# Gate and up of an encoder's feed-forward chunks computed transposed, with the inverse rms applied later

## The chip, the cores and the metric

One core of a Trainium2 chip. The metric is the device time of one execution in microseconds (us); lower is better.

## The reference

Two layers over x of shape (1, 256, 1024) in float32. Each layer has two feed-forward blocks with a mixer (spatial gating and windowed attention) between them:

```python
def _rmsnorm(x, g):
    inv = rsqrt(mean(x * x, axis=-1) + EPS)
    return (x * inv) * g

def _swiglu(h, w_in, w_out):          # w_in 1024 x 5632, w_out 2816 x 1024
    gate, up = split(h @ w_in, 2, axis=-1)
    return (silu(gate) * up) @ w_out

for l in range(2):
    x = x + 0.5 * _swiglu(_rmsnorm(x, ffn1_norm[l]), ffn1_w_in[l], ffn1_w_out[l])
    ...                               # mixer: x = x + concat(A, B) @ w_mix_out[l]
    x = x + 0.5 * _swiglu(_rmsnorm(x, ffn2_norm[l]), ffn2_w_in[l], ffn2_w_out[l])
```

## The kernel before, in words

**Arithmetic.** Every float32 operand of a large product is split in a high part (rounded to the matmul type, L464 for weights) and a low part (the rest, L689). `products` (L994) makes three matmuls for each product: high x by high w (L997), high x by low w (L998), low x by high w (L1000). x (transposed, gained, not yet divided by its rms) is the stationary operand, in pieces of 128 tokens; the weights stream, 512 columns at a time.

**Weights.** They come in units of 128 x 2048 (1 MB). SP loads a unit into one of three `raw` buffers (`load`, L293), when the low part of the unit three positions earlier is made. ScalarE (ACT) makes `w_hi`, VectorE (DVE) `w_lo`, in six slots. A chunk of the feed-forward block is 256 of the 2816 inner columns; there are 11. It has two `in` units (each with gate and up columns of four of the eight k tiles) and one `out` unit.

**A feed-forward block** (`ffn` on each engine: L510 ACT, L767 DVE, L1038 PE), four times in the kernel. For chunk c and token half t, PE computes gate and up side by side in PSUM bank `U[t]` (`enter`, L1039: 24 matmuls of 512 columns). ACT takes silu of the gate with the inverse rms as its scale (`silu`, L486), DVE multiplies by up and the inverse rms (`mul`, L705). The result h has tokens on partitions, but the next product wants it the other way: PE transposes it (`transpose_h`, L1049 to L1053: four 128 x 128 for a chunk), ACT and DVE take the high and low part (`take_hT`, L490 and L711), and `leave` (L1055) multiplies by the `out` unit into `acc` (24 matmuls of 512). PE's order for chunk c is: both halves of `enter(c)` with the transposes of h(c-1) in the middle, then `leave(c-1)`. At the end of a block come the transposes of h(10) (two before `leave(9, 0)`, two before `leave(9, 1)`), the residual (`residual`, L714, scale 0.5, L734), and the transposes of the new x (L1035), which are begun as soon as x of token half 0 is there (L1107).

**Around it.** POOL computes the inverse rms (`inverse_rms`, L405, L402 and L403) and, at the start, loads small rows from its own DMA queue (L417, L419). In the first block of layer 0, PE transposes these rows (`other_rows`, L1205 to L1209) in the middle of `enter(1, 0, ...)`, behind a wait for them. In layer 1, POOL loads `ws`, `sgain` and `sinks` (L442 to L444) behind the last inverse rms of layer 0. Orders on all engines are written out by hand.

Of the kernel before, what the change touches and what calls it, by code (L numbers as in the profile page):

```python
# [15 lines left out]
F32 = mybir.dt.float32  # L16
# [3 lines left out]
ALU = mybir.AluOpType  # L20
# [69 lines left out]
def encoder(nc, x, ffn1_norm, ffn1_w_in, ffn1_w_out, mix_norm, w_mix_in, sgu_norm, sgu_w, sgu_b,  # L90
# [18 lines left out]
    RELS = 2 * S - 1  # L109
    bias_rows = nc.dram_tensor("bias_rows", (NH, P, RELS), F32, kind="Internal").ap()  # L110

    with ExitStack() as ctx:
# [14 lines left out]
        xT_hi = sb("xT_hi", [P, KT, S], F32R)  # L127
        xT_lo = sb("xT_lo", [P, KT, S], F32R)
# [17 lines left out]
        kT_lo = hT_hi[:, 0, :, :].rearrange("p t (g n) -> p t g n", n=P)  # L146
        gv = sb("gv", [P, 2, MIX_A])
# [28 lines left out]
        U = [bank("U0"), bank("U1")]  # L176
        acc = [[bank("C0"), bank("C1")], [bank("D0"), bank("D1")]]
        C0, C1 = acc[0]
        TR = [bank("TR0"), bank("TR1")]
# [25 lines left out]
        h_done = sem("h_done")  # L205
        hT_psum = sem("hT_psum")
# [67 lines left out]

        def n_tran(L, q, t, half):

            return L * 12 + (4 * q + 2 * t + half + 1)
# [15 lines left out]
        def _(sp):  # L293
# [8 lines left out]
            def load_in(L, f, c, u, j=0):  # L302
                def parts(dst):
                    d = dst.rearrange("p (k g n) -> p k g n", k=4, g=2)
                    for g in range(2):
                        cols = bass.ds(j * (2 * FC) + (g * DFF + c * FC), FC)
                        yield d[:, :, g, :], w_in[f][bass.ds(L, 1), :, 4 * u:4 * u + 4, cols][0]
                load(L, pos_in(f, c, u), parts, j)
# [75 lines left out]
        def _(pool):  # L384
# [23 lines left out]

            def norm(L, name, c0, groups, n):
# [5 lines left out]
            inverse_rms(0, 0, 1)  # L415
            for r0, v in ((48, q_norm), (50, k_norm)):
# [22 lines left out]
            for L in range(DEPTH):  # L439
# [13 lines left out]
                for q in (2, 3) if L < DEPTH - 1 else (2,):  # L453
                    inverse_rms(L, q, 0)
                    inverse_rms(L, q, 1)
# [3 lines left out]
        def _(act):  # L459
# [16 lines left out]
            def silu(L, f, c, t, j=0):  # L476
                if t == 0:
                    act.wait_ge(gu_ready, n_gu(L, f, c, j))
                else:
                    act.wait_ge(units_used, n_used(L, pos_in(f, c, 1), j))  # L480
                if c == 0:
                    act.wait_ge(inv_done, n_inv(L, 2 * f, t))
                else:

                    act.wait_ge(h_done, n_ffn(L, f, c - 1, t, j))
                act.activation(gate[:, t, :], U[t][:, 0:FC], ACT.Silu, scale=inv[:, t:t + 1]).then_inc(silu_done, 1)  # L486

            def take_hT(L, f, c, t, j=0):
                act.wait_ge(hT_psum, n_ffn(L, f, c, t, j))
                act.activation(hT_hi[:, c % 2, :, t * P:(t + 1) * P],  # L490
                               TR[t][:, 0:FC].rearrange("p (k n) -> p k n", k=2), ACT.Copy).then_inc(hT_hi_done, 1)

# [17 lines left out]
            def ffn(L, f, after):  # L510

                def chunk(c, j=0):
                    if c > 0:
                        silu(L, f, c - 1, 1, j)
                    split(L, pos_in(f, c + 1, 0), j)
                    if c > 0:
                        take_hT(L, f, c - 1, 0, j)
                        take_hT(L, f, c - 1, 1, j)
                    silu(L, f, c, 0, j)
                    split(L, pos_in(f, c + 1, 1), j)  # L520
                    split(L, pos_out(f, c), j)
                chunk(0)
                with act.Fori(0, 4) as j:
                    chunk(1, j)
                    chunk(2, j)
                chunk(9)
                silu(L, f, 9, 1)
                split(L, pos_out(f, 10))
                take_hT(L, f, 9, 0)
                take_hT(L, f, 9, 1)  # L530
                silu(L, f, 10, 0)
                if after is not None:
                    split(L, after[0])
                silu(L, f, 10, 1)
                take_hT(L, f, 10, 0)
# [7 lines left out]
                take_hT(L, f, 10, 1)  # L543
# [133 lines left out]
        def _(dve):  # L677
# [24 lines left out]
            def mul(L, f, c, t, j=0):  # L702
# [611 lines left out]
```

## Time and profile before

| | us |
|---|---|
| median of 3 runs (918.36 to 919.03) | 918.51 |
| the profiled execution, its own time | 918.79 |
| its span | 917.0 |
| PE busy in the span | 911.9 |
| DVE busy | 524.3 |
| ACT busy | 441.9 |
| POOL busy | 54.1 |

The span is from the first to the last instruction that the profile shows; the rest of the time lies outside of it. The granted clock of TensorE is full in each of the 40 slices of the page. Matmuls are pipelined: a 128 x 512 one lasts 0.39 us in the records, but the next starts 0.23 us after it, so starts, not durations, are what to read of PE.

### The profile page before, as it was taken

Reading aid. Unit: us, or ns where it says so; the run is one execution under the profiler, and the core shown is the slowest. Engines: PE = TensorE matmul, PEld = TensorE weight load, DVE = VectorE, ACT = ScalarE, POOL = GpSimd, SP = SyncE. Lnnn points to the kernel's source line nnn. Section 1 sums busy time; section 2 is a strip of 40 time slices with the busy share of each in tenths; the row PEclk is TensorE's granted clock in tenths of the full one; section 3 lists DMA queues with packets and bytes.
Section 4 is the critical chain, followed back from the end, with each engine's and each line's share of the span. In section 5 each row is a group of like instructions: output and inputs, shape, how many; then the busy total and the mean of one; then the engine's idle time right before and its main releaser. Section 6 shows DMA issues by size and latency. Waiting matters only on the chain.

```text
span 917.0 us, 12240 instructions
## 1 busy us (share of the span) xinstructions
PE 911.9 (99%) x4422; PEld 751.7 (82%) x4422; DVE 524.3 (57%) x631; ACT 441.9 (48%) x524; POOL 54.1 (6%) x112
## 2 busy tenths in 40 slices
PE   9999999999999999999999999999999999999998
PEld 7888888887788888888888888888877888888886
DVE  5644554477967445455466445445689574554542
ACT  6444443457856345345254443443677473443530
POOL 2400000111100000000010000000110100000000
PEclk9999999999999999999999999999999999999999
DMA  8999999843174664654456645645431665564531
GB/s 281 279 195 258 177 219 249 222 139 138 61 261 160 223 214 137 224 188 154 160 201 206 231 162 182 230 149 184 138 138 48 229 204 209 184 230 153 186 118 46
DMA packets 119582, 168.88 MB, mean 184 GB/s; under 512 B 5948, under 2 KB 98424, under 8 KB 119544
## 3 DMA queue, kind: packets, MB, share of 16 engines
q1 hardware_dynamic: 117536, 163.47, 51.9%
q0 software_dynamic: 1504, 4.73, 7.5%
q8 instruction: 26, 0.43, 0.2%
q10 hardware_dynamic: 504, 0.16, 0.1%
q14 instruction: 12, 0.10, 0.0%
HBM read 165.19 MB, written 3.14 MB: 184 GB/s over the span
## 4 chain that ended last, share of the span: by engine, by line
PE 96%; DVE 2%; DMA 1%; issue 0%; ACT 0%; SPq 0%; DVEq 0%
PE U L997 19%; PE U L1000 19%; PE U L998 19%; PE C L997 6%; PE C L1000 6%; PE C L998 6%; PE D L997 5%; PE D L998 5%; PE D L1000 5%; PE TR L1052 2%; PE TR L1035 1%; DVE sc L856 1%; PE D L1179 1%; PE TR L1135 1%; DMA raw<-in_ffn_w_in_dram 1%; DVE w_lo L689 0%
## 5 line engine op out<-in xcount | busy, mean ns | idle before, releaser
L689 DVE TENSOR_TENSOR w_lo<-raw,w_hi 128x2048 fp32r<-128x2048 f32 x150 | 340.1, 2289 | 116.5 <-ACT w_hi L464 116.5
L997 PE MATMUL U<-w_hi,xT_hi 128*128 128x512 f32 (+1 forms) x784 | 307.9, 393 | 0.1
L464 ACT ACTIVATE w_hi<-raw 128x2048 fp32r<-128x2048 f32 x150 | 283.4, 1918 | 49.8 <-DMA raw<-in_ffn_w_in_dram 35.2
L1000 PE MATMUL U<-w_hi,xT_lo 128*128 128x512 f32 (+1 forms) x784 | 302.5, 386 | 0.0
L998 PE MATMUL U<-w_lo,xT_hi 128*128 128x512 f32 (+1 forms) x784 | 301.9, 385 | 0.0
L1000 PEld LDWEIGHTS U<-w_hi,xT_lo 128*128 128x128 f32 x784 | 147.3, 188 | 30.3
L997 PEld LDWEIGHTS U<-w_hi,xT_hi 128*128 128x128 f32 x784 | 147.4, 188 | 28.6 <-DVE xT_lo L750 0.3
L998 PEld LDWEIGHTS U<-w_lo,xT_hi 128*128 128x128 f32 x784 | 147.6, 188 | 27.9
L490 ACT ACTIVATE hT_hi<-TR 128x256 fp32r<-128x256 f32 x88 | 29.4, 382 | 242.9 <-PE TR L1052 242.9
L711 DVE TENSOR_TENSOR hT_lo<-TR,hT_hi 128x256 fp32r<-128x256 f32 x88 | 33.5, 419 | 167.6 <-ACT hT_hi L490 167.6
L486 ACT ACTIVATE small<-U,inv 128x256 f32<-128x256 f32 x88 | 41.8, 475 | 114.6 <-PE D L1000 78.0
L705 DVE SCALAR_TENSOR_TENSOR small<-U,inv,small 128x256 f32<-128x256 f32 x88 | 42.0, 477 | 63.2 <-ACT small L486 62.8
L997 PE MATMUL D<-w_hi,hT_hi 128*128 128x512 f32 x176 | 69.2, 393 | 0.0
L997 PE MATMUL C<-w_hi,hT_hi 128*128 128x512 f32 x176 | 68.9, 391 | 0.0
L998 PE MATMUL D<-w_lo,hT_hi 128*128 128x512 f32 x176 | 68.6, 390 | 0.0
L998 PE MATMUL C<-w_lo,hT_hi 128*128 128x512 f32 x176 | 68.5, 389 | 0.0
L1000 PE MATMUL D<-w_hi,hT_lo 128*128 128x512 f32 x176 | 55.6, 389 | 0.0
L1000 PE MATMUL C<-w_hi,hT_lo 128*128 128x512 f32 x176 | 54.3, 390 | 0.0
L1000 PEld LDWEIGHTS D<-w_hi,hT_lo 128*128 128x128 f32 x176 | 33.0, 188 | 7.0
L1000 PEld LDWEIGHTS C<-w_hi,hT_lo 128*128 128x128 f32 x176 | 33.0, 188 | 6.9
L998 PEld LDWEIGHTS C<-w_lo,hT_hi 128*128 128x128 f32 x176 | 33.1, 188 | 6.7
L997 PEld LDWEIGHTS C<-w_hi,hT_hi 128*128 128x128 f32 x176 | 33.0, 188 | 6.7
(121 smaller groups left out, 706.2 us busy)
## 6 DMA issues: line engine op xcount, KB each, us to landing
raw<-in_ffn_w_in_dram SPq DMA_DIRECT2D x168, 512.0 KB, 4.7
raw<-in_ffn_w_out_dram SPq DMA_DIRECT2D x88, 512.0 KB, 5.2
raw<-in_w_mix_in_dram SPq DMA_DIRECT2D x28, 512.0 KB, 4.7
raw<-in_w_mix_out_dram SPq DMA_DIRECT2D x16, 512.0 KB, 3.6
raw<-in_ffn_w_in_dram SPq DMA_DIRECT2D x16, 256.0 KB, 4.7
bias_rows<-brow POOLq DMA_DIRECT2D x8, 255.5 KB, 11.3
bias<-bias_rows POOLq DMA_DIRECT2D x8, 192.0 KB, 6.1
xs<-in_x_dram SPq DMA_DIRECT2D x2, 512.0 KB, 5.5
```

The source lines that it names most:

```text
L464: act.activation(w_hi[:, p % SLOTS, :], raw[:, p % RAW, :], ACT.Copy).then_inc(hi_ready, 1)
L486: act.activation(gate[:, t, :], U[t][:, 0:FC], ACT.Silu, scale=inv[:, t:t + 1]).then_inc(silu_done, 1)
L490: act.activation(hT_hi[:, c % 2, :, t * P:(t + 1) * P], TR[t][:, 0:FC].rearrange("p (k n) -> p k n", k=2), ACT.Copy).then_inc(hT_hi_done, 1)
L689: dve.tensor_tensor(w_lo[:, p % SLOTS, :], raw[:, p % RAW, :], w_hi[:, p % SLOTS, :].bitcast(F32), ALU.subtract).then_inc(lo_ready, 1)
L705: dve.scalar_tensor_tensor(out=h[:, t, :], in0=U[t][:, FC:2 * FC], scalar=inv[:, t:t + 1], in1=gate[:, t, :], op0=ALU.mult, op1=ALU.mult). ...
L711: dve.tensor_tensor(hT_lo[:, c % 2, :, cols], TR[t][:, 0:FC].rearrange("p (k n) -> p k n", k=2), hT_hi[:, c % 2, :, cols].bitcast(F32), AL ...
L856: ins = dve.tensor_tensor_reduce(sc[:, r % 2, i, :], acc[0][i % 2][:, (i // 2) * S:(i // 2 + 1) * S], bias[:, hh, (1 - t) * P:(1 - t) * P ...
L997: pe.matmul(out_, x_hi, w_hi[:, slot, c], start=start, stop=False)
L998: pe.matmul(out_, x_hi, w_lo[:, slot, c], start=False, stop=False)
L1000: last = pe.matmul(out_, x_lo, w_hi[:, slot, c], start=False, stop=stop)
L1035: last = pe.transpose(TR[half][:, i * P:(i + 1) * P], xs[:, t, k * P:(k + 1) * P], ident[:, :])
L1052: last = pe.transpose(TR[t][:, kk * P:(kk + 1) * P], h[:, t, kk * P:(kk + 1) * P], ident[:, :])
```

## The change

For chunks 1 to 10 the `in` units are laid out anew: one unit holds all eight k tiles of the gate, the other those of up (the same two DMAs of 512 KB with 1 KB pieces). The weights are stationary and x streams: `xT` holds high and low x of a k tile side by side, so `w_hi` by [high x, low x] is one matmul of 512 columns, and `w_lo` by high x one of 256. The outcome is already transposed (inner columns on partitions): gate goes to the two `U` banks, up to the two `TR` banks, and the two halves of a bank are added up by ACT (copy) and DVE (add). Because tokens are now on the free axis, the inverse rms of all tokens is spread over the partitions (through DRAM, by POOL), multiplies the gate before silu, and for up it is left out and put in the residual's scale; 0.5 goes into h. Chunk 0 is computed as before, with its four transposes.

In a chunk ACT copies the gate (128 x 512, `copy_gate`), takes its silu (128 x 512), copies each half of up (128 x 256, `copy_up`) and rounds each half of h (128 x 256, `round_h`). PE's `enter_gate(c)` waits for `gate_done` of chunk c-1 and fills the two `U` banks, `enter_up(c)` waits for `h_done` of chunk c-1 and fills the two `TR` banks; each calls `enter_T` twice.

```diff
@@ sync
             def load_in(L, f, c, u, j=0):
+                    if c == 0:
...
+                    else:
+                        d = dst.rearrange("p (k n) -> p k n", k=KT)
+                        cols = bass.ds(j * (2 * FC) + (u * DFF + c * FC), FC)
+                        for i in range(2):
+                            yield d[:, 4 * i:4 * i + 4, :], w_in[f][bass.ds(L, 1), :, 4 * i:4 * i + 4, cols][0]
@@ gpsimd
+            def spread_inverse(L, f):
+                pool.wait_ge(inv_done, n_inv(L, 2 * f, 1))
+                row = 2 * L + f
+                for t in range(2):
+                    pool.dma_start(inv_rows[row, t, :].unsqueeze(1), inv[:, t:t + 1]).then_inc(inv_stored, 16)
+                pool.wait_ge(inv_stored, 32 * (row + 1))
+                pool.dma_start(inv_b[:, :], inv_rows[row:row + 1, :, :].rearrange("a t n -> a (t n)").partition_broadcast(P)[:, 0, :]
+                               ).then_inc(inv_spread, 16)
             inverse_rms(0, 0, 0)
             inverse_rms(0, 0, 1)
+            spread_inverse(0, 0)
             for r0, v in ((48, q_norm), (50, k_norm)):
...
+                spread_inverse(L, 1)
+                if L < DEPTH - 1:
+                    inverse_rms(L, 3, 0)
+                    inverse_rms(L, 3, 1)
+                    spread_inverse(L + 1, 0)
@@ scalar
+                def chunk(c, j=0):
                     split(L, pos_in(f, c + 1, 0), j)
+                    copy_gate(L, f, c, j)
+                    silu(L, f, c, j)
+                    copy_up(L, f, c, 0, j)
                     split(L, pos_in(f, c + 1, 1), j)
+                    copy_up(L, f, c, 1, j)
+                    round_h(L, f, c, 0, j)
+                    round_h(L, f, c, 1, j)
                     split(L, pos_out(f, c), j)
@@ vector
+            def gates(L, f, c, j=0):
+                dve.wait_ge(gate_copied, n_gate(L, f, c, j))
+                dve.tensor_tensor(gate, U_pair[:, :, 0:S], gate, ALU.add).then_inc(gate_added, 1)
+                if c == 1:
+                    dve.wait_ge(inv_spread, 16 * (2 * L + f + 1))
...
+                dve.tensor_tensor(gate, gate, inv_b[:, :].unsqueeze(1).to_broadcast([P, 2, S]), ALU.mult
+                                  ).then_inc(gate_done, 1)
+            def ups(L, f, c, kk, j=0):
+                dve.tensor_tensor(h[:, kk, :], TR[kk][:, 0:S], h[:, kk, :], ALU.add).then_inc(up_added, 1)
...
+                dve.scalar_tensor_tensor(out=h[:, kk, :], in0=h[:, kk, :], scalar=0.5, in1=gate[:, kk, :],
+                                         op0=ALU.mult, op1=ALU.mult).then_inc(h_done, 1)
+            def rest_h(L, f, c, kk, j=0):
+                dve.tensor_tensor(hT_lo[:, c % 2, kk, :], h[:, kk, :], hT_hi[:, c % 2, kk, :].bitcast(F32),
+                                  ALU.subtract).then_inc(hT_lo_done, 1)
-                    dve.scalar_tensor_tensor(out=xh, in0=acc[t][half][:, :], scalar=1.0 if ph == 1 else 0.5, in1=xh,
+                    dve.scalar_tensor_tensor(out=xh, in0=acc[t][half][:, :], scalar=1.0 if ph == 1 else inv[:, t:t + 1], in1=xh,
@@ tensor
+                def enter_T(c, g, kk, j=0):
+                    p = pos_in(f, c, g)
+                    slot, to = p % SLOTS, (U, TR)[g][kk]
+                    if kk == 0:
+                        split_ready(L, p, j)
+                    for k in range(KT):
+                        cols = slice(k * FC + kk * P, k * FC + (kk + 1) * P)
+                        if k < KT - 1:
+                            pe.matmul(to, w_hi[:, slot, cols], xT[:, k, :, :], start=k == 0, stop=False)
+                        last = pe.matmul(to[:, 0:S], w_lo[:, slot, cols], xT_hi[:, k, :], start=False, stop=False)
+                        if k == KT - 1:
+                            last = pe.matmul(to, w_hi[:, slot, cols], xT[:, k, :, :], start=False, stop=True)
...
+                pe.wait_ge(h_done, n_ffn(L, f, 0, 0))
+                enter_T(1, 0, 0)
+                if L == 0 and f == 0:
+                    other_rows()
+                transpose_h(0)
+                transpose_h(1)
+                enter_T(1, 0, 1)
+                for kk in range(2):
+                    pe.wait_ge(hT_lo_done, n_ffn(L, f, 0, kk))
+                    enter_T(1, 1, kk)
...
+                leave(0, 0)
+                leave(0, 1)
                 def chunk(c, j=0):
+                    enter_gate(c, j)
+                    enter_up(c, j)
                     leave(c - 1, 0, j)
                     leave(c - 1, 1, j)
-                transpose_h(10, 0)
                 leave(9, 0)
                 leave(10, 0)
-                transpose_h(10, 1)
                 leave(9, 1)
```

## Rows read from the trace of the kernel before

**Rows 1.** The page's busy times, and the chain that ended last, by engine.

```profile
PE 911.9 (99%) x4422; PEld 751.7 (82%) x4422; DVE 524.3 (57%) x631; ACT 441.9 (48%) x524; POOL 54.1 (6%) x112
...
PE 96%; DVE 2%; DMA 1%; issue 0%; ACT 0%; SPq 0%; DVEq 0%
```

**Rows 2.** The chain in order of time: start us, us, what; transposes of two chunks following.

```profile
293.21 0.44 PE TR L1052 x4
...
310.02 0.44 PE TR L1052 x4
```

**Rows 3.** Timeline of PE: start us, us, instruction; the 24 matmuls of an `enter`.

```profile
304.42 0.39 PE L997 MATMUL U<-w_hi,xT_hi 128*128 128x512 f32 x1
...
309.86 0.60 PE L1052 MATMUL TR<-ident,small 128*128 128x128 f32 x4
```

**Rows 4.** Timeline of PE in the mixer: matmuls of 256 columns, then of 512.

```profile
204.26 0.28 PE L1000 MATMUL U<-w_hi,xT_lo 128*128 128x256 f32 x1
...
206.77 0.28 PE L1000 MATMUL U<-w_hi,xT_lo 128*128 128x256 f32 x1
206.89 0.40 PE L997 MATMUL C<-w_hi,xT_hi 128*128 128x512 f32 x1
...
207.36 0.39 PE L1000 MATMUL C<-w_hi,xT_lo 128*128 128x512 f32 x1
...
209.64 0.38 PE L1135 MATMUL TR<-ident,kd 128*128 128x128 f32 x2
```

**Rows 5.** Groups by line and shape, DVE and ACT: busy us, mean ns, idle before.

```profile
L689 DVE TENSOR_TENSOR w_lo<-raw,w_hi 128x2048 fp32r<-128x2048 f32 x150 | 340.1, 2289 | 116.5 <-ACT w_hi L464 116.5
...
L705 DVE SCALAR_TENSOR_TENSOR small<-U,inv,small 128x256 f32<-128x256 f32 x88 | 42.0, 477 | 63.2 <-ACT small L486 62.8 <-DVE gall L784 0.3
L711 DVE TENSOR_TENSOR hT_lo<-TR,hT_hi 128x256 fp32r<-128x256 f32 x88 | 33.5, 419 | 167.6 <-ACT hT_hi L490 167.6
...
L744 DVE TENSOR_TENSOR sc<-TR,gcur 128x512 f32<-128x512 f32 x24 | 15.5, 686 | 14.3 <-PE TR L1035 14.3
...
L464 ACT ACTIVATE w_hi<-raw 128x2048 fp32r<-128x2048 f32 x150 | 283.4, 1918 | 49.8 <-DMA raw<-in_ffn_w_in_dram 35.2 <-DMA raw<-in_ffn_w_out_dram 9.7 <-PE D L1000 4.1
```

**Rows 6.** The kernel's start: timelines of POOL and PE, DMA issues with KB and us to landing.

```profile
15.09 0.55 POOL L403 TENSOR_TENSOR inv<-mean,mhalf 128x1 f32<-128x1 f32 x1
15.59 0.77 POOL L417 DMA_DIRECT2D wsT<-in_q_norm_dram  x1
...
16.93 0.56 POOL L419 DMA_DIRECT2D wsT<-in_sgu_b_dram  x1
...
24.56 0.27 PE L1209 MATMUL C<-ident,wsT 60*128 60x60 f32 x1
...
wsT<-in_q_norm_dram POOLq DMA_DIRECT2D x1, 1.0 KB, 5.2
...
wsT<-in_sgu_b_dram POOLq DMA_DIRECT2D x1, 4.0 KB, 5.4
```

**Rows 7.** Timeline of PE: the same eight transposes, first and second time.

```profile
4.77 1.97 PE L1035 MATMUL TR<-ident,xs 128*128 128x128 f32 x8
...
12.68 1.04 PE L1035 MATMUL TR<-ident,xs 128*128 128x128 f32 x8
```

**Rows 8.** Timelines of DVE, PE and ACT where the other three blocks begin.

```profile
290.96 0.48 DVE L705 SCALAR_TENSOR_TENSOR small<-U,inv,small 128x256 f32<-128x256 f32 x1
...
478.61 1.92 ACT L464 ACTIVATE w_hi<-raw 128x2048 fp32r<-128x2048 f32 x1 [3.65 <-DMA raw<-in_ffn_w_in_dram]
...
479.73 0.60 PE L1052 MATMUL TR<-ident,small 128*128 128x128 f32 x4
...
743.40 1.92 ACT L464 ACTIVATE w_hi<-raw 128x2048 fp32r<-128x2048 f32 x1 [2.65 <-DMA raw<-in_ffn_w_in_dram]
...
745.12 0.60 PE L1052 MATMUL TR<-ident,small 128*128 128x128 f32 x4
```

**Rows 9.** Timelines of DVE and PE at the end of layer 0.

```profile
457.04 1.28 DVE L734 SCALAR_TENSOR_TENSOR xs<-C,xs 128x512 f32<-128x512 f32 x2
...
458.86 1.03 PE L1035 MATMUL TR<-ident,xs 128*128 128x128 f32 x8
```

More of the change, by code:

```diff
@@ L303, in parts @@
                 def parts(dst):
[L304 to L307, printed above, removed]
+                    if c == 0:
+                        d = dst.rearrange("p (k g n) -> p k g n", k=4, g=2)
+                        for g in range(2):
+                            yield d[:, :, g, :], w_in[f][L, :, 4 * u:4 * u + 4, g * DFF:g * DFF + FC]
+                    else:
[3 more added lines that the diff above has]
+                            yield d[:, 4 * i:4 * i + 4, :], w_in[f][bass.ds(L, 1), :, 4 * i:4 * i + 4, cols][0]
                 load(L, pos_in(f, c, u), parts, j)
@@ L785, in ffn @@
                     dve.sem_inc(gain_taken, 1)
+                take_hT(L, f, 0)
+                take_hT(L, f, 1)
+                split(L, pos_in(f, 2, 0))
+                gates(L, f, 1)
+                ups(L, f, 1, 0)
+                split(L, pos_in(f, 2, 1))
+                ups(L, f, 1, 1)
+                rest_h(L, f, 1, 0)
+                rest_h(L, f, 1, 1)
+                split(L, pos_out(f, 1))
                 with dve.Fori(0, 4) as j:
-                    chunk(1, j)
                     chunk(2, j)
+                    chunk(3, j)
                 if f == 0:
                     layer_gains(L)
-                chunk(9)
-                mul(L, f, 9, 1)
                 split(L, pos_out(f, 10))
-                take_hT(L, f, 9, 0)
-                take_hT(L, f, 9, 1)
-                mul(L, f, 10, 0)
+                gates(L, f, 10)
                 if after is not None:
                     split(L, after[0])
-                mul(L, f, 10, 1)
-                take_hT(L, f, 10, 0)
+                ups(L, f, 10, 0)
+                rest_h(L, f, 10, 0)
+                ups(L, f, 10, 1)
+                rest_h(L, f, 10, 1)
                 if after is None:
@@ L1018, in project, with sum_out @@
                 return last
-            def sum_out(L, p, t, lhs_hi, lhs_lo, start, stop, j=0):
+            def sum_out(L, p, t, lhs_hi, lhs_lo, start, stop, j=0, second_half=None):
                 split_ready(L, p, j)
                 for kk in range(2):
+                    if kk == 1 and second_half is not None:
+                        pe.wait_ge(hT_lo_done, second_half)
                     last = products([acc[t][0][:, :], acc[t][1][:, :]], lhs_hi(kk), lhs_lo(kk), p % SLOTS,
```

209 lines of the change are left out of this document (125 added, 84 removed).

## The prediction

> **What bounds the kernel now.** I read the page first: PE is busy 911.9 us of a span of 917.0, DVE 524.3, ACT 441.9, and the chain that ended last lies on PE for 96% [rows 1]. So what counts is the distance between PE's starts, and every place at which PE could begin to wait. Then the chain in order of time gives the period of a chunk: the transposes of one chunk and those of the next lie 310.02 - 293.21 = 16.81 us apart [rows 2]. The timeline of PE gives the pieces: from the first matmul of an `enter` to the transposes behind it, 24 matmuls of 512 columns take 309.86 - 304.42 = 5.44 us, 0.2267 us each [rows 3]. A chunk has 72, which is 16.32 us; the rest, 0.49 us, is what four transposes cost with the slower matmuls behind them.
>
> **Part 1, transposes removed.** Chunks 1 to 10 of four blocks lose them: 40 x 0.49 = -19.6 us, all on the path.
>
> **Part 2, the products turned.** Per chunk the 48 matmuls of 512 columns become 32 of 512 and 32 of 256. The columns are the same, 24,576; the matmuls and weight loads are 16 more. What a matmul of 256 costs is in the mixer: 21 of them from 204.26 to 206.77, 0.1195 us each [rows 4]. 512 columns in one piece cost 0.2267, in two 0.239, so there is a fixed part of some 0.012 us in each. But an alternation of 512 and 256 stands nowhere in the trace, so it has bounds. Below: each keeps its pace, 32 x (0.2267 + 0.1195) = 11.08 against 48 x 0.2267 = 10.88, +0.20 a chunk, +8 us for 40. Above: the 512s right behind the 256s start 0.235 apart ((207.36 - 206.89) / 2) [rows 4]; if all of them stayed there, 32 x 0.3545 = 11.34, +0.46, +18.5 us. Over the first twelve they average (209.64 - 206.89) / 12 = 0.229, which would give +0.28, +11.1. The slowness dies out by itself in a dozen, and the 256s of these rows show none of it, so I take the middle of the low bound and this average: +9.6 us. A gain below the low bound is excluded: the columns are the same and the loads more.
>
> Weight loads last 0.19 us in the records, longer than a matmul of 256 takes, yet the 256s of rows 4 run at 0.12, so loads overlap one another. The Trainium skill (TensorE: Matmul & The Clock Gate, LDWEIGHTS) gives the time of a load by its columns, which makes 107 ns for 128; by it the load would just hide behind 256 columns, and the sum would be that of the low bound.
>
> **Part 3, elementwise work.** Per chunk DVE has three splits of 2.289, two operations of 128 x 512 (0.686, as L744), and six of 128 x 256 (0.42 to 0.48, as L711 and L705): 6.87 + 1.37 + 2.6 = 10.9 us of a period of 16.6. ACT has 3 x 1.918 and the copies, silu and roundings, some 2.8 at the same prices: 8.6 us [rows 5]. Both fit. The order fits too: with gate ready at 5.5 us of a chunk and up at 8.3 and 11.1, h is split by about 15, and PE wants it for `leave` at 16.6 + 11.1; `U` and `TR` are read well before PE comes back. Splits are made over ten us ahead. Cost in the steady chunks: nothing, covered by PE's 16.6 us; without that cover it would be DVE's 10.9. The w_in DMAs keep number, size and 1 KB pieces: nothing.
>
> **Part 4, POOL's spread in the first block.** POOL has its inverse rms at 15.6 and then issues three small loads, which land 5.2 to 5.4 us after issue, though 1 to 4 KB; PE takes these rows at 24.56, not waiting [rows 6]. After the change two stores and a wait come first: issues at 15.6 and 16.4, landed at 21.6 (the price of the loads; nothing smaller and nearer is there), the broadcast issued at 21.8, then the three loads at 22.3, 23.1, 23.7; the last lands at 29.1. `other_rows` stands on PE behind `enter_T(1, 0, 0)`, that is at 24.5. PE waits 4.6 us, with all of its queue behind it. Bounds: 0, if these transfers took under 3 us each; 8, if the stores of 128 single words took twice as long. The spread itself lands at 27, and `gates(1)` wants it after 34: hidden. The same chain in the other blocks starts 14 us before `gates(1)`: hidden.
>
> The skill (DMA: Bandwidth & Descriptors, Anatomy of one DMA) has about 2 us plus bytes for a DMA issued by POOL; by it the last load would land near 22.7, and the wait would be gone. The rows of this case say 5.2, which I use.
>
> **Part 5, deadlines at the other block starts.** `transpose_h(0)` used to need h after 5.44 us of chunk 1, and ACT and DVE had until the end of both enters. Now h of token half 1 is wanted 3.0 us into chunk 1, and the low part of hT at 6.0, since up of chunk 1 goes into `TR`. Chunk 1 starts 5.44 before its transposes of rows 8.
> - Layer 0, block 2: start 287.6, h wanted at 290.6, made by 291.44 less overlap [rows 8]: 0.5 us.
> - Layer 1, block 1: start 474.3, low part wanted at 480.3. ACT splits the unit before, which lands only at 478.6; 1.9 + 0.4 + 0.4 later makes 481.2: 0.9 us. The broadcast and the 0.5 MB of `ws` and `sgain` are now moved into the time of this load: up to 1.8 us more at the 350 GB/s that it gets. I take 1.9 us.
> - Layer 1, block 2: start 739.7, h wanted at 742.7, made by 743.5 (0.6 us); then 743.4 + 1.9 + 0.8 = 746.1 for the low part, wanted at 746.3: 0.9 us with the broadcast beside it.
>
> **Part 6, the block ends.** Transposes of h(10) are counted in part 1. At the end of layer 0 four half splits stand before the residual, and they now begin behind copy, add, multiply and round instead of silu and one `take_hT`, about 1.0 later, less 0.34 for the `take_hT` that is gone: the residual starts at 457.7 in place of 457.04 and takes 1.28; PE wants x at 458.86 - 0.46 = 458.4 [rows 9]. Cost 0.7 us. Elsewhere the residual has over 0.5 us to spare.
>
> **The sum.** -19.6 + 9.6 + 4.6 + 0.5 + 1.9 + 0.9 + 0.7 = -1.4. The profiled execution took 918.79, 0.28 above the median of 918.51. Against the median this gives 917.1.
>
> A measurement of this kernel can tell about 0.2% from no change, 1.8 us: below 916.7 is faster, above 920.3 slower.
>
> **Rivals.**
> *The wait for the small rows isn't there or is mostly hidden* (transfers land in about 2 us): 917.1 - 4.6 = 912.5. For: DMA is idle from 20 to 22 us. Against: all small loads of POOL's queue took over 5. Chance 0.18, faster.
> *The alternation is slow all along* (the disturbed pace of the 512s stays, because a 256 renews it each time): at the average +11.1 it is 918.6, at the high bound 917.1 + 8.9 = 926. It decides from a pace of 0.231, where the 40 chunks cost 4.1 more than I took (each 0.001 us is 1.3 us): 921.2. For: the pace right behind the 256s. Against: it dies out. Chance 0.14, slower.
> *PE's clock falls during the wait at 24.5 us.* The eight transposes took 1.97 us at 4.8, when PE had just begun, and 1.04 at 12.7 [rows 7]: the first at 1.2 GHz, the second at 2.4. Five us of work at the low level would lose 2.5: 919.6, and with the low-level work behind a longer wait 921. The skill (TensorE: Matmul & The Clock Gate, "Why this matters for your kernels") warns that idle gaps of PE bring the low clock back; no idle gap of this size stands in this trace. Chance 0.13, half slower, half no change.
> *The change doesn't remove what it should*, because DVE falls behind in the steady chunks: 10.9 of 16.6 us speaks against; 0.02, slower.
>
> **Chances.** The forecast has 0.53. Inside it the low bound of part 2 gives 915.5 and the average 918.6, so about 0.18 of it is below 916.7 and 0.32 is no change, 0.03 above. Faster 0.18 + 0.18 = 0.36; same 0.32 + 0.06 + a little = 0.39; slower 0.03 + 0.14 + 0.06 + 0.02 = 0.25. The forecast alone spans 914.5 to 919.5. The range for 8 in 10 takes in most of the first rival and the slower cases near their point of decision: 912.5 to 922.
>
> **What would show it.** A chunk's period of 16.5 to 16.6 us, no transposes but 16 for h; if it is 16.8, part 2 is wrong. A gap on PE before L1209's successor, from about 24.5 to 29, released by a DMA of POOL's queue; if it is under 2 us, part 4 is wrong. Gaps of 0.5 to 2 us before the transposes or the first `TR` matmul of three blocks, and one of 0.7 before the x transposes at the end of layer 0. DVE near 613 us busy (524 + 40 x 2.2). A granted clock under full in the slice of the first wait would speak for the third rival. Gaps of PE inside steady chunks would make the whole forecast wrong.

## The result: 3.4% slower, and the profile after

The changed kernel takes **949.91 us** (median of 4 runs, 947.64 to 950.49) against 918.58 for the kernel before on the same chip (918.36 to 919.03): ratio 1.0336, interval 1.0317 to 1.0354. The forecast of 917.1 and its range of 912.5 to 922.0 are missed by a wide margin. The profiled execution took 950.49, its span is 948.7, 31.7 us more than before.

The page of the changed kernel, its lines on busy time, the granted clock by slices, the chain, and the groups of the two splitting engines (busy us, mean ns, idle before):

```profile
PE 917.6 (97%) x4902; PEld 774.5 (82%) x4902; DVE 612.0 (65%) x791; ACT 490.3 (52%) x604; POOL 54.9 (6%) x124
...
PEclk9799999999999999999999999999999989999999
...
PE 84%; DMA 6%; DVE 5%; ACT 3%; issue 2%; SPq 1%; ACTq 0%; DVEq 0%
...
L765 DVE TENSOR_TENSOR w_lo<-raw,w_hi 128x2048 fp32r<-128x2048 f32 x150 | 340.4, 2289 | 124.0 <-ACT w_hi L507 123.9
L507 ACT ACTIVATE w_hi<-raw 128x2048 fp32r<-128x2048 f32 x150 | 282.5, 1906 | 64.1 <-DMA raw<-in_ffn_w_in_dram 45.4
```

Against [rows 1] PE is busy 5.7 us longer, but the chain has fallen from 96% to 84% on PE and now holds DMA, DVE and ACT: the time went into waits. The granted clock has a dip in two slices; before it was full. ACT waits 45.4 us for `w_in` units, 35.2 before [rows 5]. Waits of PE are given here from the start of one matmul to the start of the next, so each contains an ordinary step of 0.23 us. DVE's 612.0 is what the forecast gave (613).

To see where, I took the start of the first `leave` product of each block as a mark. Between marks inside one block (nine chunks) the time fell from 151.33 to 150.47, four times: -3.4 us. The rest grew: the kernel's start by 13.8, layer 0's stretch between its blocks by 8.5 (114.09 to 122.62), layer 0 to layer 1 by 5.9 (35.35 to 41.24), layer 1's stretch by 7.2 (114.05 to 121.29); the end gave back 0.3. These add up to 31.7. So the steady chunks gained a little, and the four stretches in which a block begins lost 35 (for three of them, together with the end of the block before).

**The steady chunk.** It now takes 16.72 us (150.47 / 9), before 16.81 [rows 2]. PE's timeline of the changed kernel, inside a turned group:

```profile
376.04 0.39 PE L1173 MATMUL U<-xT,w_hi 128*128 128x512 f32 x1
376.26 0.28 PE L1174 MATMUL U<-xT,w_lo 128*128 128x256 f32 x1
376.38 0.40 PE L1173 MATMUL U<-xT,w_hi 128*128 128x512 f32 x1
376.61 0.28 PE L1174 MATMUL U<-xT,w_lo 128*128 128x256 f32 x1
376.73 0.40 PE L1173 MATMUL U<-xT,w_hi 128*128 128x512 f32 x1
```

A pair starts every 0.354 us by the medians, not every 0.346. Over 1120 neighbours of either kind, a 512 holds the next 256 off by a median of 0.236 us and a 256 the next 512 by 0.118. The 512's 0.236 never dies out, as it did among pure 512s in [rows 4].

**The first block.** PE, then POOL, at the kernel's start:

```profile
23.71 0.39 PE L1176 MATMUL U<-xT,w_hi 128*128 128x512 f32 x1
36.24 0.33 PE L1346 MATMUL C<-ident,wsT 60*128 60x60 f32 x1 [12.14 <-issue]
...
37.84 0.41 PE L1174 MATMUL U<-xT,w_lo 128*128 128x256 f32 x1
38.05 0.63 PE L1173 MATMUL U<-xT,w_hi 128*128 128x512 f32 x1
38.48 0.41 PE L1174 MATMUL U<-xT,w_lo 128*128 128x256 f32 x1
```

```profile
15.16 1.30 POOL L442 DMA_DIRECT2D inv_rows<-inv  x2 [0.30 <-POOL inv L431]
28.00 0.55 POOL L444 DMA_DIRECT2D inv_b<-inv_rows  x1 [11.55 <-DMA inv_rows<-inv]
28.64 0.60 POOL L456 DMA_DIRECT2D wsT<-in_q_norm_dram  x1
...
29.82 0.55 POOL L458 DMA_DIRECT2D wsT<-in_sgu_b_dram  x1
```

POOL waits 11.55 us for 1 KB of stores to land; the three small loads go out behind them, and PE stands for 12.5 us (the last of these rows lands at 29.82 + 6.33 = 36.15) where before it took them at once at 24.56 [rows 6]. Behind the gap a pair takes 38.48 - 37.84 = 0.64 us instead of 0.354; the granted clock from 36 to 40 us is 0.50, the lower of its two levels (1.2 GHz).

The stores also hold back work that doesn't wait for them. Stretches of the changed kernel (PE, PEld, DVE, ACT, POOL busy, granted clock, DMA share, GB/s):

```profile
16.00:20.00 4.00, 4.00 (x20) 3.30 (x19) 2.17 (x1) 3.97 (x4) 0.46 (x1) 1.00 1.02 353
20.00:24.00 4.00, 4.00 (x22) 3.27 (x20) 2.74 (x3) 1.38 (x1) 0.00 (x0) 1.00 0.09 16
24.00:28.00 4.00, 0.10 (x1) 0.00 (x0) 0.00 (x0) 0.80 (x1) 0.00 (x0) 0.88 0.33 54
28.00:32.00 4.00, 0.00 (x0) 0.00 (x0) 2.63 (x2) 1.48 (x2) 3.84 (x10) 0.50 0.77 182
```

The stores were issued at 15.16 and 15.90; until 20 us the loads that were already under way move at the full rate. Weight units were issued from 20.36 on, yet the DMA engines move 16 and 54 GB/s for eight microseconds; once the stores are down they move 182 and more.

**The other block starts.** ACT and PE where layer 0's second block begins, SP's queue, and from the view of DMA from 293 to 316 us the issues with median us to landing:

```profile
303.14 0.46 ACT L526 ACTIVATE small<-U,inv 128x256 f32<-128x256 f32 x1
310.46 1.91 ACT L507 ACTIVATE w_hi<-raw 128x2048 fp32r<-128x2048 f32 x1 [6.86 <-DMA raw<-in_ffn_w_in_dram]
312.28 0.64 ACT L548 ACTIVATE hT_hi<-TR 128x256 fp32r<-128x256 f32 x2
```

```profile
309.22 0.39 PE L1176 MATMUL U<-xT,w_hi 128*128 128x512 f32 x1
313.16 0.50 PE L1173 MATMUL TR<-xT,w_hi 128*128 128x512 f32 x1 [3.54 <-DVE hT_lo L787]
```

```profile
300.40 4.52 SPq L323 DMA_DIRECT2D raw<-in_ffn_w_in_dram  x4
```

```profile
inv_b<-inv_rows POOLq DMA_DIRECT2D x1, 128.0 KB, 6.6
inv_rows<-inv POOLq DMA_DIRECT2D x2, 0.5 KB, 9.3
...
raw<-in_ffn_w_in_dram SPq DMA_DIRECT2D x5, 512.0 KB, 8.6
```

A unit consists of two loads of 512 KB; the one issued from 300.40 is complete at 310.4, and ACT starts on it at 310.46. ACT waits for it with `take_hT` behind it in its order; PE's `TR` products need the low part of hT, so PE waits 3.94 us, though nothing that it wants depends on that unit. Layer 1's blocks have the same (3.8 and 4.0 us), and behind each the clock is low again. The stretches of work at the low clock come to 16.9 us in all; by 0.64 against 0.354 for a pair, some 7.5 us of them are loss, an estimate from these two paces.

**The block ends.** Layer 0's first block, and the end of layer 0:

```profile
193.73 1.92 ACT L507 ACTIVATE w_hi<-raw 128x2048 fp32r<-128x2048 f32 x1 [3.55 <-DMA raw<-in_w_mix_in_dram]
```

```profile
201.60 0.50 PE L1108 MATMUL C<-w_hi,hT_hi 128*128 128x512 f32 x1 [0.90 <-DVE hT_lo L812]
...
208.29 1.10 PE L1148 MATMUL TR<-ident,xs 128*128 128x128 f32 x8 [0.62 <-DVE xs L836]
```

```profile
479.85 1.09 PE L1148 MATMUL TR<-ident,xs 128*128 128x128 f32 x8 [0.61 <-DVE xs L836]
```

The x transposes start 1.0 us behind the last product in both places, 0.8 more than an ordinary step; in layer 0's first block PE also waits 1.3 + 0.2 for the low part of h(10), whose chain began late because ACT's `copy_gate(10)` stands behind the split of the mixer's first unit, and that unit lands only at 193.7.

### The profile page after: what moved, and what is told of

It is laid out like the page before. It is cut to its first block, busy times and chain, and to the rows that moved or that the text cites. A ratio compares the mean times of both kernels' runs of the same rounds, so it can differ in the third digit from the quotient of the medians.

```text
span 948.7 us, 13688 instructions
## 1 busy us (share of the span) xinstructions
PE 917.6 (97%) x4902; PEld 774.5 (82%) x4902; DVE 612.0 (65%) x791; ACT 490.3 (52%) x604; POOL 54.9 (6%) x124
## 4 chain that ended last, share of the span: by engine, by line
PE 84%; DMA 6%; DVE 5%; ACT 3%; issue 2%; SPq 1%; ACTq 0%; DVEq 0%
PE TR L1173 14%; PE U L1173 12%; PE TR L1174 8%; PE U L1174 7%; PE C L1108 5%; PE C L1111 5%; PE C L1109 5%; PE D L1108 5%; PE D L1111 5%; PE D L1109 5%; DMA raw<-in_ffn_w_in_dram 3%; PE TR L1176 2%; DVE w_lo L765 2%; ACT w_hi L507 2%; PE U L1176 2%; PE U L1108 2%
## 5 line engine op out<-in xcount | busy, mean ns | idle before, releaser
L507 ACT ACTIVATE w_hi<-raw 128x2048 fp32r<-128x2048 f32 x150 | 282.5, 1906 | 64.1 <-DMA raw<-in_ffn_w_in_dram 45.4
L1173 PE MATMUL TR<-xT,w_hi 128*128 128x512 f32 x560 | 206.3, 406 | 10.5 <-DVE hT_lo L787 10.5
L1173 PE MATMUL U<-xT,w_hi 128*128 128x512 f32 x560 | 202.5, 400 | 0.0
L1174 PE MATMUL TR<-xT,w_lo 128*128 128x256 f32 x640 | 169.2, 285 | 0.0
L1174 PE MATMUL U<-xT,w_lo 128*128 128x256 f32 x640 | 167.4, 282 | 0.0
L1173 PEld LDWEIGHTS TR<-xT,w_hi 128*128 128x128 f32 x560 | 108.1, 193 | 34.1 <-DVE hT_lo L787 11.5
L1174 PEld LDWEIGHTS TR<-xT,w_lo 128*128 128x128 f32 x640 | 123.8, 193 | 7.5
L1174 PEld LDWEIGHTS U<-xT,w_lo 128*128 128x128 f32 x640 | 121.8, 190 | 6.9
L1173 PEld LDWEIGHTS U<-xT,w_hi 128*128 128x128 f32 x560 | 106.3, 190 | 23.4
L803 DVE TENSOR_TENSOR small<-TR,small 128x256 f32<-128x256 f32 x80 | 33.7, 421 | 48.2 <-ACT small L540 48.2
L1108 PE MATMUL U<-w_hi,xT 128*128 128x512 f32 (+1 forms) x144 | 54.6, 380 | 0.0
```

The costliest lines, as they stand in the source:

```text
L507: act.activation(w_hi[:, p % SLOTS, :], raw[:, p % RAW, :], ACT.Copy).then_inc(hi_ready, 1)
L803: dve.tensor_tensor(h[:, kk, :], TR[kk][:, 0:S], h[:, kk, :], ALU.add).then_inc(up_added, 1)
L1108: pe.matmul(out_, x_hi, w_hi[:, slot, c], start=start, stop=False)
L1173: pe.matmul(to, w_hi[:, slot, cols], xT[:, k, :, :], start=k == 0, stop=False)
L1174: last = pe.matmul(to[:, 0:S], w_lo[:, slot, cols], xT_hi[:, k, :], start=False, stop=False)
```

## Experiments

The kernel before was run beside them on the same chip each time (medians 918.2 to 918.5). Times of this family scatter by 1 to 6 us from run to run, those of the kernel before by about 1.

The changed kernel itself was not run again, so what an edit does to it is read against its four runs of 947.6 to 950.5. The traces show how far that misleads. The three stretches in which blocks 2 to 4 begin, between the marks above, are together 21.6 us longer in the changed kernel than in the kernel before. They are 13.3 us longer in the run that only moves the first block's spread, 14.7 in the one that only groups the products, and 13.7 in the one with stores and no broadcast. At layer 0's second block, the loads of 512 KB beside the stores land after 8.3 to 9.5 us in the changed kernel, after 6.1 to 8.2 in those three. The first of these edits doesn't touch the three stretches at all, so the edits don't explain it, and the cause is not shown. So some 8 us of each difference from 949.91 can't be credited to the edit; comparisons among the experiments are free of this: with ACT's old order and two stores, their stretches lie at 13.3 to 14.7.

### The spread in the kernel before, and the small rows first

The first adds `spread_inverse` and its four calls to the kernel before, result unused. The second moves one call in the changed kernel:

```diff
             inverse_rms(0, 0, 1)
-            spread_inverse(0, 0)
...
             pool.dma_start(rows[52:60, :], sgu_b ...).then_inc(head_rows_loaded, 16)
+            spread_inverse(0, 0)
```

> The kernel before with nothing added but POOL's spread of the inverse rms (two stores of 128 single words, a wait, a broadcast, at the four places of the change); its result is not used. Theory A: the stores of single words hold up the DMA engines, so POOL's next loads and the weight units behind them come late. Then the first wait on PE (for the small rows) is some 12 us with 2 us lost to the low clock, and the unit that lands 5.2 us after its issue at the start of block 2 of layer 0 takes 9 to 10: 932 to 937 us. Theory B: only POOL waits for its stores, the weights land as before (5 to 6 us) and their lateness in the changed kernel has another source: 932 us, all of it in the first block. If neither, 919.

Measured: 931.66, ratio 1.0148 (1.0131 to 1.0164). PE stands from 24.12 to 34.42, before its transposes of the rows, then works at the low clock:

```profile
24.12 0.39 PE L1022 MATMUL U<-w_hi,xT_lo 128*128 128x512 f32 x1
34.42 0.33 PE L1231 MATMUL C<-ident,wsT 60*128 60x60 f32 x1 [9.91 <-issue]
...
35.27 0.63 PE L1020 MATMUL U<-w_lo,xT_hi 128*128 128x512 f32 x1
35.70 0.63 PE L1022 MATMUL U<-w_hi,xT_lo 128*128 128x512 f32 x1
```

That is all it costs, and both theories allow the time: the other boundaries keep their length. But a `w_in` unit issued beside the stores at 297.11 lands only after 8.3 us there too, which is theory A's sign and not B's; the old order has room for it.

> The changed kernel with the spread of the first block issued behind the three small row loads. Theory B (only the queue order on POOL costs the 12.5 us before the rows' transposes): PE's wait there goes and 13 to 15 us come back, 935 to 937. Theory A (the stores hold up the weights too): the wait only changes its name, since the units that ACT and DVE need ahead of h land late as well: 946 to 950.

Measured: 933.94, ratio 1.0157 (1.0135 to 1.018). The gap before the rows is gone, and the time is near theory B's. The mechanism is not: by the profiled executions (948.7 and 934.9 us of span) the kernel's start, where the edit is, gives back 5.5 us, and 8.3 come from the later block starts, which it doesn't touch. In the first block PE now waits 2.2 us for h and 4.4 for the low part of hT:

```profile
26.45 0.44 PE L1161 MATMUL TR<-ident,small 128*128 128x128 f32 x2 [1.92 <-DVE small L781]
33.75 0.80 PE L1173 MATMUL TR<-xT,w_hi 128*128 128x512 f32 x1 [4.05 <-DVE hT_lo L787]
```

So the row wait was the longest, and late weight units stood right behind it, as theory A says for this block.

### ScalarE's order at the block start

```diff
-                split(L, pos_in(f, 2, 0))
                 take_hT(L, f, 0)
                 take_hT(L, f, 1)
+                split(L, pos_in(f, 2, 0))
                 copy_gate(L, f, 1)
```

> The changed kernel with ACT's two copies of h transposed put ahead of its split of the next gate unit at each block start. Theory: the 3.6 to 3.9 us that PE waits before its first matmul into TR in blocks 2, 3 and 4 come from ACT standing in order behind a unit that has not landed. Then they go, and with them the low clock behind them (some 1.7, 1.7 and 3.8 us): 949.9 - 17 = 933, between 931 and 937. Rival: PE waits for something else at that point (the h products themselves): under 4 us gained, 946 or more.

Measured: 930.78, ratio 1.0134 (1.0117 to 1.0151). The three waits of 3.9 us and the low clock behind them are gone; 0.9 us for h stays at two starts; the first block still has its wait, 11.1 us. The starts of blocks 2 to 4 now cost 4.4 us over the kernel before. With the slow stores still there, this one move of ACT takes back 9 to 10 us of them by the two runs that have the same order as the changed kernel there (13.3 and 14.7), 17 by the changed kernel itself.

### The products grouped by width

```diff
-  per k: 512 (w_hi), 256 (w_lo)
+  k = 0..6: 512 (w_hi); k = 0..7: 256 (w_lo); k = 7: 512 (w_hi)
```

> The changed kernel with the 15 other matmuls of each accumulation in two runs, seven of 512 columns and then eight of 256, the last one of 512 behind them. Theory P: a 256 renews the slow pace of the 512 behind it (0.236 us in the changed kernel against 0.227), so runs of equal size cost less: the chunk's period falls from 16.72 to about 16.5, 940 to 943 us. Rival Q: the slow pace belongs to the turned products (weights stationary, x streamed), whatever the order: period 16.7, 948 to 951 us.

Measured: 937.29, ratio 1.0194 (1.0174 to 1.0213); the chunk takes 16.61 us, as theory P has it, and the time is below its range. The last kernel of this section, which has this order too, shows seven 512s in 374.51 - 372.90 = 1.61 and eight 256s in 0.95:

```profile
372.90 1.77 PE L1162 MATMUL U<-xT,w_hi 128*128 128x512 f32 x7
374.51 1.12 PE L1164 MATMUL U<-xT,w_lo 128*128 128x256 f32 x8
375.46 0.40 PE L1165 MATMUL U<-xT,w_hi 128*128 128x512 f32 x1
```

Alternation costs 0.11 us a chunk, 4.4 us for 40. The remainder of the 12.6 us under the changed kernel is shorter waits (11.0 before the rows, 2.2 to 2.8 at the block starts) and less work at the low clock; they lie in the 8 us spoken of above, and I don't credit them to the order.

### The spread without any transfer

TensorE can do it: the inverse column, repeated along the free axis, as the stationary operand, times the identity, puts `inv` along the free axis of all partitions.

```diff
+                pe.wait_ge(inv_done, n_inv(L, 2 * f, 1))
+                for t in range(2):
+                    last = pe.matmul(acc[1][1][:, t * P:(t + 1) * P],
+                                     inv[:, t:t + 1].to_broadcast([P, P]), ident[:, :], ...)
+                last.then_inc(inv_psum, 1)
                 enter_T(1, 0, 1)
...
+                dve.wait_ge(inv_psum, 2 * L + f + 1)
+                dve.tensor_copy(inv_b[:, :], acc[1][1][:, 0:S]).then_inc(inv_spread, 1)
                 gates(L, f, 1)
```

> The changed kernel, with the spread of the inverse made by TensorE: two products of the inverse column (repeated along the free axis) with the identity, into a free bank, and one VectorE copy; no small store, no broadcast. Theory A (the stores of 2 x 128 single words, while they are in flight, hold up both the small rows and the weight unit of SP's queue): the 12.5 us before the other rows, the three waits of about 3.9 us at the block starts and the low clock behind all four go; the h waits of 0.9 us and the 1.3 us at the end of layer 0's second block stay. 949.9 - 12.5 - 2.2 - 3 x 3.9 - 6.8 + about 2 for the eight small products = 918 to 920. Theory B (ACT's order alone, hT behind the split of the next unit, makes the waits at the block starts, and the turned products need that unit earlier than before): only the 14.7 us of the first block go, 935 to 937.

Measured: 923.66, ratio 1.0058 (1.0043 to 1.0073). 26 of the 31 us are gone with the transfers, ACT's order left as it was. It is 4 to 6 us above what was expected: h waits of 2.0, 0.9 and 0.9, with the low clock behind the first.

> The kernel with TensorE's spread, and the two stores of 128 single words put back at each of the four places (nobody reads what they store; POOL waits for their landing; no broadcast). Theory A (the stores hold up the weight units): the waits at the three block starts are back at 3 to 4 us each, with the low clock behind them, and the small rows of the first block wait for at least 7 us: 935 to 945. Theory C (the 128 KB broadcast or its place in POOL's queue did it, the stores cost only their own latency): the block starts have no wait before the first up product, only the first block's rows wait: 922 to 929.

Measured: 938.95, ratio 1.0223 (1.0205 to 1.0242): the stores alone, read by nobody, bring back 15.3 us, with 10.4 us before the rows and waits at the block starts, as theory A has it. The other 11.0 us to the changed kernel (949.91 - 938.95) are not shown to be the broadcast's: the two kernels above that have the broadcast lose the same at the starts of blocks 2 to 4 (13.3 and 14.7) as this one without it (13.7).

> TensorE's spread together with ScalarE's take of hT ahead of its split of the next unit at the block start. Theory A: the unit is no longer late, so the order is worth nothing or nearly so: within 1 us of the kernel with TensorE's spread alone (918 to 920). Theory B: 4 to 8 us below that kernel, and the waits that were left at the block starts go here alone.

Measured: 923.71, ratio 1.0063 (1.0049 to 1.0078). Equal: ACT's order costs nothing once units land in time, and it was worth 9 us or more beside the stores.

### What it is about the stores

One store in place of two; then, in its place, a row of the same 512 bytes out of one partition; then the single words from ScalarE's queue.

```diff
-                for t in range(2):
+                for t in range(1):
                     pool.dma_start(inv_rows[row, t, :].unsqueeze(1), inv[:, t:t + 1]).then_inc(inv_stored, 16)
```

```diff
-                    pool.dma_start(inv_rows[row, t, :].unsqueeze(1), inv[:, t:t + 1]).then_inc(inv_stored, 16)
+                pool.dma_start(inv_rows[row, 0:1, :], ident[0:1, :]).then_inc(inv_stored, 16)
```

```diff
                 silu_rows(L, f, 0)
+                act.wait_ge(inv_done, n_inv(L, 2 * f, 1))
+                act.dma_start(inv_rows[2 * L + f, 0, :].unsqueeze(1), inv[:, 0:1]).then_inc(inv_stored, 16)
```

> TensorE's spread with one store of 128 single words at each of the four places, in place of two. Theory A (the single words themselves hold up the other queue, in proportion to their number): the weight units issued behind the store land about half as late as with two (6.7 us there, 4.0 with none: about 5.4), the wait of 1.6 to 4 us before the first up product of a block goes or falls under 1 us, and the rows of the first block are waited for some 5 us rather than 10: 928 to 933, between 923.7 (no store) and 939.0 (two). Theory D (a store of any size on POOL's queue costs a fixed time): 936 to 940, as with two.

Measured: 938.04, ratio 1.0229 (1.0209 to 1.025). Half the words, the whole price (938.95 with both): the proportional theory falls, and a fixed cost for any store (theory D) is left to be tested.

> TensorE's spread, and at each of the four places one store of the same 512 bytes on POOL's queue, from one partition (a row of the identity, nobody reads it) in place of one word from each of 128 partitions. Theory W (the single words are what is slow): the store lands in 2 to 5 us, weight units behind it land in 4 to 5 us, and the time is that of no store, 923 to 925, plus at most 2 us of waiting for the first block's rows. Theory D (any write to memory on POOL's queue holds up the loads for a fixed time): 936 to 940, as with one or two stores of single words.

Measured: 923.89, ratio 1.0057 (1.004 to 1.0074), the time of no store at all: theory D falls too. PE waits 2.4 us for the small rows, in place of the 2.0 for h.

> TensorE's spread, and the one store of 128 single words at each block start issued from ScalarE's queue in place of POOL's, behind its first silu. Theory W: the store still takes 8 to 10 us to land and the weight units issued behind it are as late as with POOL's store (6 to 8 us), with waits before the first up product of 1.5 to 4 us: 928 to 936 (the first block's small rows are no longer behind it). Theory Q (POOL's queue is the cause, whose descriptors are written when the instruction runs): weight units land in 4 to 5 us, 923 to 926.

Measured: 942.77, ratio 1.0271 (1.0247 to 1.0294): more than theory W's range, and 4.7 more than the one store from POOL's queue. This store is also issued nearer to the weight units (3.1 us ahead of them where layer 0's second block starts, 5.7 with POOL's), so the difference is not shown to be the queue's. The landing times, first one row per store, then single words on POOL's queue (two stores, then one), then on ACT's:

```profile
DMA to landing us min/median/max: 1.6/2.2/5.1
```

```profile
DMA to landing us min/median/max: 5.6/8.4/10.6
```

```profile
DMA to landing us min/median/max: 8.8/9.7/10.5
```

```profile
DMA to landing us min/median/max: 7.8/8.1/9.0
```

Where layer 0's second block starts (288 to 306 us), the loads' median us to landing, and stretches with columns as above, each time first with the row store and then with ACT's store of words:

```profile
raw<-in_ffn_w_in_dram SPq DMA_DIRECT2D x6, 512.0 KB, 4.0
```

```profile
raw<-in_ffn_w_in_dram SPq DMA_DIRECT2D x4, 512.0 KB, 8.8
```

```profile
290.00:294.00 4.00, 4.00 (x23) 3.41 (x22) 3.57 (x2) 2.56 (x3) 0.00 (x0) 1.00 0.84 262
294.00:298.00 4.00, 3.35 (x22) 2.80 (x22) 2.60 (x5) 2.46 (x3) 0.00 (x0) 1.00 1.04 338
```

```profile
290.00:294.00 4.00, 4.00 (x20) 3.34 (x19) 3.04 (x3) 3.99 (x4) 0.00 (x0) 1.00 0.34 26
294.00:298.00 4.00, 3.35 (x23) 2.75 (x22) 3.27 (x3) 0.56 (x2) 0.00 (x0) 1.00 0.39 38
```

What matters is the shape of the transfer, 128 words of 4 bytes from 128 partitions, not its bytes (equal); it happens from either queue, and one is as bad as two. Whether it is the 128 partitions on the reading side or the 4-byte pieces on the writing side is open, since the row store changes both. In these stretches, with such a store in flight until 296.24, the DMA engines move 26 to 38 GB/s instead of 262 to 338, and the loads of 512 KB land after 8.3 to 8.8 us instead of 4.0 to 4.5. The trace has the 144 packets of ACT's store between 289.1 and 289.3, 1 us behind its issue at 288.25, so seven of its 8 us pass behind them. The row store had landed four microseconds before these loads were issued; it stood beside loads only in the first block, where it took 5.1 us and the loads landed as in the kernel before. The Trainium skill (DMA: Bandwidth & Descriptors, Specifications) says that a transfer under 512 bytes is written by read-modify-write, and (Rules for kernel authors) that a last dimension that isn't contiguous becomes one descriptor per element. The store here is nearest to the second: its last dimension is one word, and the trace has more packets of 4 bytes for it (144) than it has words (128). The runs agree that this shape is slow, by 2.2 against 8 to 10 us; no run shows a read-modify-write. That loads of another queue are held up meanwhile is in neither sentence and is what the runs add. By what mechanism, and why one store is as dear as two, was not settled.

### Mending the order, and everything together

```diff
                 split(L, pos_in(f, 1, 1))
-                split(L, pos_out(f, 0))
                 silu_rows(L, f, 1)
+                split(L, pos_out(f, 0))
```

VectorE's list has the same swap. It stands on TensorE's spread with hT first.

> TensorE's spread with hT ahead of the split, and chunk 0's second row tile (silu and product) ahead of the split of the first out unit on ScalarE and VectorE. If the 0.9 us waits for h before its transposes at the block starts (2.3 us in the first block) come from that split standing ahead in both queues: these four waits go, 923.7 - 0.9 x 3 - 2.3 = 918 to 920. If the wait then only moves to the first leave products, which need that unit: 922 to 924.

Measured: 918.88, ratio 1.0005 (0.9995 to 1.0014). The h waits are gone, and none came in their place at the block starts (the 1.0 us before the x transposes is still there); the time is that of the kernel before.

> TensorE's spread, hT ahead of the split, the 512-column products of a group together (seven, then the eight of 256 columns, then the last of 512), and at chunk 10 the split of the mixer's first unit behind the gate and up work on ScalarE and VectorE. If the account of where the time went is whole (start, block starts, pace, ends): the chunk takes 16.61 us in place of 16.81, 32 x 0.2 = 6.4 less over the steady chunks, 1 us of waits at the ends gone, 2 us of small products and 2 us of h waits more than before: 913 to 917, under the kernel before. If the splitting engines now become late elsewhere: 918 to 924.

Measured: 923.33 (919.88 to 926.12), ratio 1.0059 (1.0041 to 1.0077); this kernel has TensorE's spread, hT first and the grouped products, and at chunk 10 both splits of the mixer's units behind the gate and up work, without the swap above. The chunk takes 16.61. The time lies in the upper of the two ranges expected. The x transposes now wait 1.7 us at the end of each layer's first block, since the residual stands on VectorE behind both splits; in layer 1 that wait is new. The trace is that of its fastest run, 919.88, and the spread of its runs, 6 us, I can't explain from it.

> All the repairs together: TensorE's spread, hT and the second row tile ahead of the splits, products grouped by width, and at the block ends chunk 10's work ahead of the mixer's first unit, and the residual of the first row tile ahead of the second unit's split. If the account is whole, the four h waits (about 5 us), the waits of 1.0 to 1.7 us before the x transposes and the 0.8 us in the last leave are gone, and the chunk takes 16.61 in place of 16.81: 912 to 916, below the kernel before. If the splits that were put back are late for the mixer's first products: 917 to 921.

```diff
                 rest_h(L, f, 10, 1)
+                split(L, after[0])
+                residual(L, 2 * f, 0)
                 split(L, after[1])
-                residual(L, 2 * f, 0)
```

At the end of layer 0, where the next layer's first two units are split, the residual is moved ahead of the second one in the same way.

Measured: **913.47** (913.35 to 916.28, 5 runs), ratio **0.9953** (0.9939 to 0.9966): faster than both kernels. Its page, busy time, clock and chain:

```profile
PE 905.5 (99%) x4918; PEld 769.9 (84%) x4918; DVE 613.5 (67%) x795; ACT 490.4 (54%) x604; POOL 56.6 (6%) x112
...
PEclk9999999999999999999999999999999999999999
...
PE 91%; DVE 6%; ACT 1%; DMA 1%; issue 0%; SPq 0%; DVEq 0%; ACTq 0%
```

PE has 6.4 us less work than in the kernel before [rows 1], and 0.67 us of wait is left at each mixer's start.

## Why the prediction was wrong, point by point

- **Part 4** is the step that failed worst. I priced two stores of 128 single words by the nearest DMAs of the trace, loads of 1 to 4 KB at 5.2 us, and doubled that for the upper bound of the wait. They took 9.7 and 11.8 us in the first block, the wait was 12.5 us in place of 4.6, and 2 us of low clock came behind it. The bound was also added up wrong: stores twice as long put everything behind them off by 5.2, which makes 9.8 and not 8; the measured wait is beyond that too. Worse was the sentence "The same chain in the other blocks starts 14 us before `gates(1)`: hidden". It asked only when the *result* is wanted. The stores cost through what they do to weight units in flight, and those the new order needs. Without the transfers of the spread 26.3 of the 31.3 us are gone (949.91 - 923.66); the two stores alone, put back, cost 15.3 (938.95 - 923.66), and some 8 of the rest are in the runs of the changed kernel alone, unexplained.
- **Part 5**, 3.3 us in sum, took the landing of units from the trace of before, plus 1.8 us for bandwidth in one block. It named the right chain (unit, ACT's split, hT, `TR` products), yet for layer 0's second block looked at h alone. Measured 4.9 in layer 0, 3.8 and 4.9 in layer 1: 13.5 us, and the low clock behind. The kernel with hT first and the one with TensorE's spread alone show that ACT's order and the late units are both needed for the waits before the `TR` products: take away either, and they are gone.
- **The clock** I held as a rival at 0.13, behind the first wait alone. It fell at all four block starts, 7.5 us by the estimate above. Behind the first wait the price was right (4.4 us of work at the low level, 2.0 lost, where I had five and 2.5); the other three places I didn't have. The 1.97 us of [rows 7], from which I took the low level, stand in a stretch for which the profile gives the full clock (4 to 6 us of the kernel before), so they didn't show it; the pairs of 0.64 us at a granted clock of 0.50 do.
- **Part 2** was mis-sized. By the medians above a group of 16 takes 7 x 0.236 + 6 x 0.118 + 0.119 + 0.118 + 0.227 = 2.82 us, four of them 11.30, and with the period measured it is +0.40 over 10.88 a chunk where I took 0.24: +16 us for 40 instead of +9.6. I argued that the 512s' slowness dies out; that was a reading of pure 512s. Grouped by width the 512s start 0.230 apart, alternating 0.236, so it is a 256 ahead that renews it. The rival "slow all along" was right; by itself it would have made the forecast 923.5.
- **Part 1** held: 16.81 - 0.49 + 0.40 is 16.72, the period measured. **Part 3** held: DVE 612.0 against 613, no wait inside a steady chunk.
- **Part 6**: the x transposes at the end of layer 0 came 0.8 late (I said 0.7). "Elsewhere the residual has over 0.5 us to spare" failed in layer 0's first block, 2.5 us in all: I had moved elementwise work ahead on ACT without asking what it stood behind.

Added up, the run is 32.8 us above the forecast. The row wait has 7.9 of them, the other block starts 10.2, the clock 7.5, the pace 6.4 and the block ends 2.8 (3.5 against 0.7), together 34.8; the ordinary steps inside the nine waits, 2.1, make up the difference.

With the spread free of transfers the forecast's other terms give 912.5, and the run 923.7. Pace (6.4), small products (4 x 0.43 = 1.7), ends (2.8 against 0.7) and starts with one low stretch (5.3 against 3.3) make 12.2 of these 11.2 us, so that the account closes within 1 us.

## What to carry to other kernels

Before a transfer is called hidden, ask what other transfers it shares the time with, and who waits for those: a store of a column as 128 single words costs not only its own landing time but that of the loads beside it, so put a per-partition scalar along the free axis with a matmul against the identity. And when a step is turned so that its operands are wanted earlier, redraw the in-order lists of the engines that prepare them: here one swap in two lists gave 4.8 us (923.71 to 918.88), the turned products in the steady chunks 3.4.

## What was not expected of the hardware

- 512 bytes stored as 128 words of 4 bytes, one from each partition: medians of 8 to 10 us to landing, one store or two, from either queue, while all DMA of the core falls to 26 to 38 GB/s; the same bytes from one partition: 2.2 us (5.1 beside loads in flight), and no load lands later.
- Alternating matmuls of 512 and 256 columns with a new weight each: 0.236 us behind a 512, 0.118 behind a 256; in groups 0.230 and 0.119.
- In these traces the granted clock fell behind every wait of PE of 3.8 us and more; between 2.0 and 3.6 us it went either way (behind 2.0 it fell with TensorE's spread alone, behind the 3.6 that began at 300.6 with ScalarE's store it didn't); behind a single one of 0.9 to 1.8 it didn't.
